# Solved blocks stored in 16 transfers in place of 64, and one sum of squares a batch later

## The reference, cut to what matters

```python
# group A: 8 heads of 64, own chunk of 64 tokens + 8 before it
q, k = rms_norm(q, q_g), rms_norm(k, k_g)
scores = q @ k.T * Dh ** -0.5 + bias          # masked outside the band
out = softmax(scores) @ v                     # later rms_norm over all 512 columns
# group B: 4 heads of 128, gated delta rule, chunkwise
L = tril(kb @ kc.T * decay, -1)
sol = triangular_solve(I + L, [vb, kb * exp(gc)])
for chunk: v_new = u - w @ S; o = qd @ S + intra @ v_new; S = S * decay + kd.T @ v_new
# both: norm, concat, output projection, residual, RMSNorm, SwiGLU FFN of 2816, residual
```

## Time and profile before

| what | value |
|---|---|
| time, median of 3 runs | 1295.24 us (1295.04 to 1296.6) |
| the profiled execution's own time | 1294.48 us |
| its span in the trace | 1292.7 us |
| granted TensorE clock, mean | 0.997 of full |
| PE busy | 1269.5 us, 98% |
| DVE / ACT / POOL busy | 58% / 45% / 59% |
| chain that ended last | PE 80%, DVE 7%, ACT 4%, POOL 3%, ACTq 2% |
| DMA packets under 512 B | 20936 of 77807 |

### The profile page before, as it was taken

The page is one execution under the profiler, slowest core; times in us unless marked ns, Lnnn a source line. Parts: engine busy times, 40 slices in busy tenths (PEclk is TensorE's granted clock), DMA queues, the critical chain, the costliest instruction groups (busy, mean ns, idle before and its releaser), DMA issues.

```text
span 1292.7 us, 18300 instructions
## 1 busy us (share of the span) xinstructions
PE 1269.5 (98%) x6908; PEld 1064.6 (82%) x6908; DVE 749.7 (58%) x1035; ACT 580.8 (45%) x932; POOL 759.0 (59%) x515
## 2 busy tenths in 40 slices
PE   8999999999989999999999999999999999999999
PEld 8888888888878788988887888888888888888887
DVE  5556556756816766744586665656545656445552
ACT  6587555562126655552353332333333324654441
POOL 5444576764425572233257996898778884754541
PEclk9999999999999999999999999999999999999999
DMA  5711355431143004452111555433344437986663
GB/s 183 261 49 40 104 142 146 140 88 45 37 102 140 2 18 155 156 198 112 65 66 66 187 187 202 170 146 119 146 187 188 163 114 255 317 303 192 196 194 147
DMA packets 77807, 185.10 MB, mean 143 GB/s; under 512 B 20936, under 2 KB 25104, under 8 KB 70680
## 3 DMA queue, kind: packets, MB, share of 16 engines
q1 hardware_dynamic: 72000, 180.19, 40.9%
q10 hardware_dynamic: 5720, 3.74, 1.0%
HBM read 129.58 MB, written 56.94 MB: 144 GB/s over the span
## 4 chain that ended last, share of the span: by engine, by line
PE 80%; DVE 7%; ACT 4%; POOL 3%; issue 2%; ACTq 2%; DMA 1%; POOLq 0%; DVEq 0%
PE ps L2232 29%; PE ps L2257 16%; PE ps L389 15%; PE ps L412 7%; PE ps L2049 2%; ACTq L649 2%; DVE YB L1479 2%; DVE TMP L1476 1%; DVE SX L1810 1%; PE ps L2083 1%; PE ps L2071 1%; PE ps L2142 1%; PE ps L374 1%; PE ps L2029 1%; POOL WR L836 1%
## 5 line engine op out<-in xcount | busy, mean ns | idle before, releaser
L389 PE MATMUL ps<-HT,SPLIT 128*128 128x512 f32 (+1 forms) x1392 | 317.5, 385 | 0.0
L389 PEld LDWEIGHTS ps<-HT,SPLIT 128*128 128x128 f32 x1392 | 252.5, 188 | 49.4
L2257 PE MATMUL ps<-S,HI 128*128 128x512 f32 x616 | 189.4, 389 | 0.0
L1015 POOL TENSOR_TENSOR S<-RAB,S 128x512 fp32r<-128x512 f32 x77 | 107.8, 1405 | 90.5 <-ACT S L1186 90.2
L2257 PEld LDWEIGHTS ps<-S,HI 128*128 128x128 f32 x616 | 115.7, 188 | 23.9
L2232 PE MATMUL ps<-S,WR 128*128 128x512 f32 x516 | 120.5, 389 | 0.4 <-POOL WR L836 0.4
L2257 PE MATMUL ps<-S,LO 128*128 128x512 f32 x308 | 119.8, 389 | 0.0
L1688 DVE TENSOR_TENSOR LO<-RAB,HI 128x512 fp32r<-128x512 f32 x77 | 65.1, 854 | 92.0 <-ACT HI L1183 92.0
L2232 PE MATMUL ps<-HI,WR 128*128 128x512 f32 x360 | 115.0, 390 | 0.2 <-POOL WR L836 0.2
L2232 PEld LDWEIGHTS ps<-S,WR 128*128 128x128 f32 x516 | 96.8, 188 | 20.9 <-POOL WR L836 0.8
L2232 PE MATMUL ps<-HI,WX 128*128 128x512 f32 x344 | 112.7, 389 | 0.6 <-ACT UV L1151 0.6
(11 more groups left out here) (285 smaller groups left out, 2572.3 us busy)
## 6 DMA issues: line engine op xcount, KB each, us to landing
hidden<-HB SPq DMA_DIRECT2D x11, 1792.0 KB, 6.6
RAB<-hidden SPq DMA_DIRECT2D x77, 256.0 KB, 3.0
RAW<-units SPq DMA_DIRECT2D x36, 512.0 KB, 3.9
RAWG<-w_gate SPq DMA_DIRECT2D x11, 1024.0 KB, 10.8
RAWU<-w_up SPq DMA_DIRECT2D x11, 1024.0 KB, 5.0
RAWD<-w_down SPq DMA_DIRECT2D x11, 1024.0 KB, 8.8
down_t<-RAWD SPq DMA_DIRECT2D x11, 1024.0 KB, 4.1
RAB<-down_t SPq DMA_DIRECT2D x44, 256.0 KB, 4.0
```

The lines of the kernel that those rows point to most:

```text
L389: mm = pe.matmul(ps[:, bank + a // HALF, a % HALF:a % HALF + width], w, right[other][:, k, a:a + width], start=(k == order[0] and part == ...
L1015: pool.tensor_tensor(down_b(q, 1), RAB[:, q % RAWS, 1, :], down_b(q, 0).bitcast(F32), ALU.subtract).then_inc(R["b_lo"], 1)
L2257: mm = pe.matmul(ps[:, bank + t, :], down_a(q, part)[:, t * P:(t + 1) * P], down_b(q, other), start=(p == 0 and i in (1, 6, 5, 7) and part ...
```

## The change

- `blocks_store` writes 16 partitions with each transfer, 64 KB, so that 8 transfers store `YB` and 8 store `TMP`. So that the 128 blocks lie at one even step in DRAM, each head's 128x128 matrix gets a tensor area of its own with one row of 128 numbers behind it (129 rows); block g then begins at g * 4128 numbers.
- The zeros written before are 516 numbers wide in place of 512.
- `ring_load` reads `TT` and `UT` head by head: 4 pieces of 512 B for each partition in place of one of 2 KB.
- SP issues the first bias load after all its 8 stores; before, 16 of 32 stores stood ahead of it. ACT issues 4 stores after tile 24 and 4 after tile 25.
- `att_acc(0)` moves from the head of DVE's step 13 to that of step 14. `att_acc(1)` stays in step 18.

```diff
-ACC_STEP = {BATCH_OF[LAST_OF[j]] + 5: j - 1 for j in range(1, NPAIR - 1)}
+ACC_STEP = {BATCH_OF[LAST_OF[1]] + 6: 0, BATCH_OF[LAST_OF[2]] + 5: 1}
...
-BIAS_AFTER = 3
+STORES = 8
+DIAG = BLOCK * P + BLOCK
+HEAD_AT = (P // BLOCK) * DIAG
...
-        zeros = PROJ[:, Q0, 0:HALF]
+        zeros = PROJ[:, Q0, 0:NHD * HEAD_AT // P]
...
-                for m in range(NT):
-                    blocks_store(sp, YB, solved, m)
-                    if m == BIAS_AFTER:
-                        sp.wait_ge(ext_out, 32)
-                        sp.wait_ge(split_done, U_OUT)
-                        sp.dma_start(bias_of(0), bias_rows[0].rearrange("s p c -> p s c")).then_inc(bias_in[0], 16)
-
-            def blocks_store(eng, tile, dst, m):
-
-                step = P // BLOCK
-                for h in range(NHD):
-                    first = (m * NHD + h) * step
-                    eng.dma_start(bass.AP(dst.tensor, m * P * NHD * P + h * P,
-                                          [[BLOCK * NHD * P + BLOCK, step], [NHD * P, BLOCK], [1, BLOCK]]),
-                                  tile[first:first + step, :, :]).then_inc(S["block_out"], 16)
+                for part in range(STORES):
+                    blocks_store(sp, YB, solved, part)
+                sp.wait_ge(ext_out, 32)
+                sp.wait_ge(split_done, U_OUT)
+                sp.dma_start(bias_of(0), bias_rows[0].rearrange("s p c -> p s c")).then_inc(bias_in[0], 16)
+
+            def blocks_store(eng, tile, dst, part):
+
+                n = P // STORES
+                eng.dma_start(bass.AP(dst.tensor, part * n * DIAG, [[DIAG, n], [P, BLOCK], [1, BLOCK]]),
+                              tile[part * n:(part + 1) * n, :, :]).then_inc(S["block_out"], 16)
...
+                def load_heads(tile, src, done):
+                    sp.dma_start(tile[:, m % 2, :, :], bass.AP(src.tensor, m * NHD * HEAD_AT, [[P, P], [HEAD_AT, NHD], [1, P]])
+                                 ).then_inc(done[m % 2], 16)
...
-                load(TT, solved_t[m], ring_in)
+                load_heads(TT, solved_t, ring_in)
...
-                load(UT, solved[m], ring_in)
+                load_heads(UT, solved, ring_in)
...
-                        act.wait_ge(S["block_out"], 16 * 4 * NT + 32 * NT * NHD)
+                        act.wait_ge(S["block_out"], 16 * 4 * NT + 32 * STORES)
...
-                        for m in range(4 * (t - Z0), 4 * (t - Z0) + 4):
-                            blocks_store(act, TMP, solved_t, m)
+                        for part in range((t - Z0) * STORES // 2, (t - Z0 + 1) * STORES // 2):
+                            blocks_store(act, TMP, solved_t, part)
```

More of the change, by code:

```diff
@@ L711, in _ @@
                 sp.wait_ge(S["keys_out"], 32 * NT)
-                sp.wait_ge(S["block_out"], 16 * 4 * NT + 32 * NT * NHD)
+                sp.wait_ge(S["block_out"], 16 * 4 * NT + 32 * STORES)
                 for m in range(2):
@@ L2461 @@
     blocks = nc.dram_tensor("blocks", (P, BLOCK * BLOCK), F32, kind="Internal").ap()
-    solved = nc.dram_tensor("solved", (NT, P, NHD * P), F32, kind="Internal").ap()
-    solved_t = nc.dram_tensor("solved_t", (NT, P, NHD * P), F32, kind="Internal").ap()
+    solved = nc.dram_tensor("solved", (NT, P, NHD * HEAD_AT // P), F32, kind="Internal").ap()
+    solved_t = nc.dram_tensor("solved_t", (NT, P, NHD * HEAD_AT // P), F32, kind="Internal").ap()
     pre = nc.dram_tensor("pre", (NT, 4, P, NHD * P), F32, kind="Internal").ap()
```

## The result

| | before | after |
|---|---|---|
| median time | 1295.14 us (1293.62 to 1296.6, 4 runs) | 1287.82 us (1286.1 to 1288.43, 4 runs) |
| ratio | | 0.994, 95% interval 0.9927 to 0.9953 |
| the profiled execution, time and span | 1294.48 and 1292.7 us | 1287.71 and 1286.0 us |

A forecast was written before the change was run, and what follows sets the result against it. It took PE to bound the kernel, with 4.54 us of reachable idle time behind ACT's late stores. Terms of 6.2 + 1.0 = 7.2 us gave 1288.0 us from the median (82%), range 1286.4 to 1291.0.

The forecast's parts named there:

- first term: PE's wait before batch 2's scores: 6.2 us gained, 4.5 idle time and 1.7 clock; bounds 4.5 and 6.5.
- second term: DVE's steps 13 and 14: moving the addition gains 1.9 us, costs 0.85, net 1.0; otherwise 0 or 1.9.
- The threshold: ACT's last store must land by 373.5 for all of the gain; each us later takes one away.
- two bounds: Stores' transfers: unchanged at 27 us, landing near 379, or 10.8 us by DMA share, landing near 364; the second taken.
- The table load: ACT's exponential table load stands behind the wait for the first maximum, 374.53; DVE has its inverse at 377.6.
- The second rival: PE between the scores of batches 2 and 3: clock falls to 0.50, 1.7 us lost, 1289.7 us; 5%.
- The sum: Whole kernel: 6.2 + 1.0 = 7.2 us gained, profiled execution 1287.3 us, 1288.0 us from the median.
- The bias load and the ring loads: Bias load issued no later than before; `TT` and `UT` loads land 0.2 us later, hidden: nothing.
- third rival: Delta rule: 512-byte loads land in 10 us, PE waits 4.4 us before tiles 3 to 7, 1310 us; 2%.
- The zeros: Zeros 0.8% wider: 0.1 us more, hidden by 8.6 us of slack of the unit load behind them.
- fourth rival: Zeros' rows of 2064 B written at half the rate: stage 10.3 us longer, 1.7 us late, 1289.7 us; 3%.
- The first rival: Stores' 128 B pieces go at the old rate: last landing near 379, batch 2's gain gone, 1294.2 us; 8%.

The follow-up runs named there:

- e3: The changed kernel with the blocks stored in 64 transfers of 4 partitions each, still into the padded layout: 1292.89 us.
- e4: The changed kernel with the blocks stored in 64 transfers of 16 KB, each over 16 partitions and 8 of the 32 rows: 1287.55 us.
- e9: The changed kernel itself, without an edit, run again beside its variants: 1287.63 us.
- e1: The changed kernel with the first addition of squares back at DVE's step 13: 1290.29 us.
- e2: The kernel before with only the first addition of squares moved to DVE's step 14: 1292.7 us.
- e6: The changed kernel with the second addition of squares moved from DVE's step 18 to 19: 1286.59 us.
- e8: The changed kernel with the zeros written in rows of 2048 bytes in place of 2064: 1286.51 us. Its table sorts fourteen profiles by row size.
- e11: The changed kernel with the second addition of squares at step 19 and 12 filling transposes in PE's 1.36 us gap: 1286.74 us.
- e12: The changed kernel with the first addition of squares moved from the head to the middle of DVE's step 14: 1288.01 us.
- e10: The changed kernel with the second addition of squares at step 19 and zeros in rows of 2048 bytes, the gap left open: 1286.21 us.

## Why the prediction was right

The time came out at 1287.82 us against 1288.0, and at 1287.71 for the profiled execution against 1287.3. The total is better than its terms, and that is luck: the first term came out 1.3 us too large in the first profile, the second 0.8 us too small.

**The threshold and the stores: right.** The forecast was a last landing near 364. ACT's last issue ends at 360.5, its stores land 3.9 us after issue by the median, and tile 26 is done at 367.29 without a wait for a DMA. Of the two bounds, the one from the DMA share (0.40 leaves a factor of 2.5) was the true one. The price of an issue was off: 0.86 to 0.93 us, where "the row of the same piece count" gave 0.56, for pieces of 512 B. With 13 us of room up to 373.5 it cost nothing. e3 and e4 show that the number of partitions is what counts.

**The table load: wrong, harmless.** I had it behind the wait for the first maximum, at 374.5, and the inverse at 377.6. It ran at 368.33, right behind tile 26, and the inverse came at 376.44. PE was the limit in either case, as forecast.

**The first term, 6.2 us: the mechanism right, the size from 6.5 down to 4.9.** At batch 2 DVE stands 6.24 us earlier, as worked out; PE starts the scores at 381.81 (forecast 381.8). At batch 3, before lost another 0.26 us to its own low clock (395.15 - 390.18 = 4.97 us from batch to batch, 4.71 in e9), so that the full term is 6.5, the upper bound that I gave. e9's profiled execution shows it: with a start 0.33 us later, which comes from the zeros' stage, it biases batch 4 at 394.39, before at 400.56, 6.17 + 0.33 = 6.50 (DVE's timeline of before, then of e9). In the changed kernel's first profile the low clock after the gap takes 1.6 us of that back: batch 4 begins at 395.66, 4.90 us earlier than before.

```profile
395.15 0.82 DVE L1810 CUSTOM_DVE_ANT_0 SX<-ps,BIAS 128x640 f32<-128x640 f32 x1 [1.24 <-PE ps L2049]
400.56 0.69 DVE L1810 CUSTOM_DVE_ANT_0 SX<-ps,BIAS 128x512 f32<-128x512 f32 x1 [1.76 <-issue]
...
442.72 0.82 DVE L1810 CUSTOM_DVE_ANT_0 SX<-ps,BIAS 128x640 f32<-128x640 f32 x1 [1.24 <-PE ps L2049]
```
```profile
384.27 0.82 DVE L1812 CUSTOM_DVE_ANT_0 SX<-ps,BIAS 128x640 f32<-128x640 f32 x1 [2.12 <-PE ps L2051]
388.98 0.82 DVE L1812 CUSTOM_DVE_ANT_0 SX<-ps,BIAS 128x640 f32<-128x640 f32 x1 [1.24 <-PE ps L2051]
394.39 0.69 DVE L1812 CUSTOM_DVE_ANT_0 SX<-ps,BIAS 128x512 f32<-128x512 f32 x1 [1.75 <-issue]
```

The step that failed is "with no idle time in which the clock fell before": a single gap was taken out, and the one behind it was then the next at which the clock can fall. **The second rival** named the place and had 5%; it comes about in the first profile, at 1.6 us where it had 1.7, and by the mean clock in 6 of 9 executions. It was put too low because before's 1.36 us gap did no harm. But until shortly before that gap PE had been at the low level, up to 391.1, and one profile of the kernel before can't say how often a gap does harm: that kernel's larger gap, the 1.76 us at step 13, which the prediction doesn't mention, did none there and was followed by the low clock in e1.

**The second term, 1.0 us: mis-sized, it is 1.83.** The sentence that failed is "I take the 2.05 of the neighbouring place". Up to step 12 the shift is 4.89 us (442.72 - 437.83), from step 13 on 6.72: 1.83 us. The other value that stood there, 1.22 and a term of 1.9, was the right one, and e2 alone gives 1.8 as well. What decides is POOL. Before, the addition began at 447.38 while POOL's two scalings ran from 444.52 to 448.35; it ended 1.08 us after them. After, it began at 447.22, ahead of POOL's 447.45, took 1.21, and POOL's two scalings took 4.74 us where two of 1.90 make 3.8 (the excess is in the first, 2.73 us). In e1, at step 13, with POOL at work since 440.14 for 3.83 us, it is 2.05 again:

```profile
443.01 2.05 DVE L1512 TENSOR_TENSOR PROJ<-PROJ 128x1024 f32<-128x1024 f32 x1 [1.50 <-ACT PROJ L1087]
```

The step, the square and the number of the pair are thus no explanation: e6's second addition has no wait ahead of it and takes 2.13 us beside POOL's split. At step 18, before and after, it is the same: POOL's instruction ends at 476.89 and 470.18, the addition at 477.98 and 471.26. In all five cases the addition ends 1.08 or 1.09 us after the POOL instruction that it met, so its length is what was left of that instruction, 0.96 to 1.05 us, and 1.08 more. The conversion of the squares (e8's table) does the same with 0.46 to 1.65 us left: it ends 0.55 or 0.56 us after POOL's instruction in e1, e3, e4, e9, e11 and e12. The Trainium skill, page "SBUF — State Buffer", section "SBUF: two separate sides", has this as a rule: DVE and GpSimd share one pair of ports, "an exclusive lock, not a bandwidth split", and whichever starts first keeps it for its whole instruction. The additions named here agree, and the rule read against POOL's timeline would have given the right term: before, POOL is idle from 448.35 to 454.17, and step 14 begins at 454.02. It was seen on both sides, but no run moved DVE's side on purpose; e12 was meant to.

**The sum.** 6.5 - 1.6 + 1.83 = 6.7 us in the first profile (time 6.77 less); without the fall 6.5 + 1.83 = 8.3, less the later start of 0.33, makes 8.0 in e9's (1294.48 - 1286.43 = 8.05).

**The bias load and the ring loads: nothing, as forecast.** The bias load was issued at 360.09 (before: 361.34). SP was done with its stores at 358.15, though, not at 355.7, and then waited for POOL's last split, which ended at 360.01: the wait that the prediction took for over is the one that sets this issue now. Ring loads landed 0.1 us later by the median of eight for `TT` (3.7 to 3.8) and 0.3 for `UT` (2.9 to 3.2; in the tiles of the earlier trace rows 2.5 to 3.2), in place of 0.2, and the wait ahead of L2144 stayed as it was. So the third rival, from a landing of 7.1 us on, was far off.

**The zeros: the cost wrong, and "hidden" only by chance.** "0.1 us more" became 2.0 to 4.3 us of lateness for POOL in the ten profiles with rows of 2064 bytes; the fourth rival's half rate was nearer in kind. The slack of 8.6 us was measured to the wrong place, PE's use of that unit at 76.77. What comes sooner is DVE's conversion of the squares at 73.5 us, beside which POOL must have nothing left to do: a start of POOL up to 65.23 cost nothing, from 65.75 on PE lost time (e8's table). In the first profile it was nothing, in e9's 0.45 us. With rows of 2048 bytes 1.6 of the 2 us of the first profile are gone again, and PE loses nothing (e8, e10).

**The first rival**, that the pieces set the time, is refuted by e4: the same pieces in as many transfers, and the gain is there.

## What to carry to other kernels

A store that is slow with a low DMA share is asked first how many partitions each of its transfers touches: 16 in place of 4 was worth all of the stores' gain, whatever the number of transfers and with pieces of 128 B unchanged. Before a duration is taken from a neighbouring row, look at what POOL does beside both places: DVE's addition here had one price beside a working POOL and another beside an idle one. The same goes for slack: a late POOL can reach PE through a DVE instruction that never reads what POOL makes. And where a large gap of TensorE goes, look for the next smaller one behind it: the clock may now fall there, in some executions and not in others, so one profile doesn't settle it.

## What was not expected of the hardware

- **A gap of 1.36 us of TensorE** is followed by 3.4 us at 1.2 GHz in the changed kernel's first profile and by nothing in e9's; by the mean clock of each run it is 6 of 9 runs against 3. What decides isn't known. The moment doesn't: in e6 and e10 the gap lies at the same place of the profile, 385.86 to 387.22, and the clock held in e6 and fell in e10. With the gap filled it held in 15 of 15.
- **The addition of 128x1024 numbers** took 1.20 to 1.22 us or 2.05 to 2.14, in the same kernel, and the conversion of as many 0.69 to 2.20. The wait for POOL is inside these durations; the profile shows no idle time for it.
- **Rows of 2064 in place of 2048 bytes**: 0.8% more bytes, and the landing of such a store of zeros went from 9.0 to 11.1 us, the rate from 42 to 46 us from 408 GB/s to 342 (312 in e9; 391 in e8). Whether the size of the row or its alignment does it, e8 doesn't tell apart.
